# A chunked recurrence's 16x16 block inverses: from TensorE squarings to VectorE arithmetic through a DRAM scratch, with the grams of all head groups ahead

## The reference, cut to what matters

```python
def step(s, x):                       # s: one 64x64 state per head, 16 heads
    r, w, k, v, a, b = x              # one token
    sa = jnp.einsum("hij,hj->hi", s, a)
    s = s * w[:, None, :] + sa[..., None] * b[:, None, :] + v[..., None] * k[:, None, :]
    return s, jnp.einsum("hij,hj->hi", s, r)
```

## Time and profile before

| | |
|---|---|
| median of 3 runs | 1138.67 us |
| span of the profiled execution | 1140.1 us |
| TensorE busy | 1100.6 us, 97% |
| VectorE busy | 819.5 us, 72% |
| ScalarE busy | 574.0 us, 50% |
| recurrence, first half (groups 0 and 1) | 366.0 to 423.4 us |
| recurrence, second half (groups 2 and 3) | 423.4 to 476.4 us |

### The profile page before, as it was taken

One profiled execution on the slowest core, in us unless ns is written; L12 is line 12 of the kernel. 1 busy time (PEld: TensorE's weight loads), 2 busy tenths in 40 slices (PEclk: granted clock), 3 DMA queues, 4 the chain that ended last, 5 costly groups with the idle time before them and its releaser, 6 DMA issues.

```text
span 1140.1 us, 20465 instructions
## 1 busy us (share of the span) xinstructions
PE 1100.6 (97%) x8356; PEld 932.2 (82%) x8356; DVE 819.5 (72%) x1150; ACT 574.0 (50%) x736; POOL 42.0 (4%) x48
## 2 busy tenths in 40 slices
PE   9999999999999896899999999999999999999997
PEld 7888888889777586777888888798987788999996
DVE  4665554558398545878999997999999977555554
ACT  5645543355565443464433447456576656444443
POOL 0000000000001310100111100000000000000000
PEclk9999999999999989999999999999999999999999
DMA  9585555643243101287999964555440454555533
GB/s 330 192 264 185 176 178 198 215 161 122 94 132 125 48 21 42 85 274 253 356 344 350 354 226 140 165 179 185 149 160 14 155 182 143 185 193 175 204 128 112
DMA packets 129236, 204.89 MB, mean 180 GB/s; under 512 B 11192, under 2 KB 86733, under 8 KB 129166
## 3 DMA queue, kind: packets, MB, share of 16 engines
q1 hardware_dynamic: 121732, 176.58, 47.2%
q0 software_dynamic: 6560, 25.19, 6.4%
q10 hardware_dynamic: 874, 2.12, 0.5%
HBM read 201.78 MB, written 1.05 MB: 178 GB/s over the span
## 4 chain that ended last, share of the span: by engine, by line
PE 79%; DVE 13%; DMA 3%; ACT 3%; issue 2%; SPq 0%; ACTq 0%; DVEq 0%
PE ps L698 22%; PE ps L700 22%; PE ps L699 22%; PE ps L1144 3%; DVE wl L2532 2%; DVE wide L3219 2%; DMA raw<-in_ffn_w_up 2%; PE ps L924 1%; DMA raw<-in_ab_w_in 1%; PE ps L775 1%; PE ps L1057 1%; PE ps L1176 1%; PE ps L1449 1%; PE ps L1056 1%; PE ps L1081 1%
## 5 line engine op out<-in xcount | busy, mean ns | idle before, releaser
L2532 DVE TENSOR_TENSOR wl<-raw,wh 128x2048 fp32r<-128x2048 f32 (+2 forms) x154 | 345.3, 2247 | 97.5 <-ACT wh L1740 97.2
L698 PE MATMUL ps<-wh,xh 128*128 128x512 f32 (+3 forms) x856 | 335.7, 392 | 4.3 <-DVE wl L2532 2.3
L700 PE MATMUL ps<-wl,xh 128*128 128x512 f32 (+3 forms) x856 | 328.3, 384 | 0.0
L699 PE MATMUL ps<-wh,xl 128*128 128x512 f32 (+3 forms) x856 | 327.9, 383 | 0.0
L1740 ACT ACTIVATE wh<-raw 128x2048 fp32r<-128x2048 f32 (+2 forms) x154 | 287.0, 1878 | 52.6 <-PE ps L700 30.2
L698 PEld LDWEIGHTS ps<-wh,xh 128*128 128x128 f32 x856 | 160.9, 188 | 39.4 <-issue 3.4
L700 PEld LDWEIGHTS ps<-wl,xh 128*128 128x128 f32 x856 | 160.8, 188 | 31.8
L699 PEld LDWEIGHTS ps<-wh,xl 128*128 128x128 f32 x856 | 161.0, 188 | 30.2 <-issue 1.0
L698 PE MATMUL ps<-wh,gh 128*128 128x512 f32 x288 | 112.7, 391 | 0.8 <-DVE wl L2532 0.8
L699 PE MATMUL ps<-wh,gl 128*128 128x512 f32 x288 | 112.3, 390 | 0.0
L700 PE MATMUL ps<-wl,gh 128*128 128x512 f32 x288 | 112.1, 389 | 0.0
(11 more groups left out here) (423 smaller groups left out, 1367.7 us busy)
## 6 DMA issues: line engine op xcount, KB each, us to landing
wide<-in_w_ada POOLq DMA_DIRECT2D x24, 1024.0 KB, 10.1
raw<-in_ffn_w_gate SPq DMA_DIRECT2D x44, 512.0 KB, 4.3
raw<-in_ffn_w_up SPq DMA_DIRECT2D x44, 512.0 KB, 5.5
raw<-in_ffn_w_down SPq DMA_DIRECT2D x22, 1024.0 KB, 5.1
raw<-in_w_mlp_in SPq DMA_DIRECT2D x16, 1024.0 KB, 7.2
raw<-in_w_mlp_out SPq DMA_DIRECT2D x16, 1024.0 KB, 5.2
raw<-in_w_in SPq DMA_DIRECT2D x16, 512.0 KB, 4.9
raw<-in_w_in SPq DMA_DIRECT2D x8, 1024.0 KB, 5.1
```

What stands on the lines that cost most here:

```text
L698: pe.matmul(o, lh, rh, start=start, stop=False)
L699: pe.matmul(o, ll, rh, start=False, stop=False)
L700: return pe.matmul(o, lh, rl, start=False, stop=stop)
L2532: v.tensor_tensor(wl[:, s, 0:width], raw[:, s, 0:width], f32(wh[:, s, 0:width]), ALU.subtract).then_inc(lo_ready[s], 1)
```

## The change

- `power2` to `inverse` are gone on TensorE, and with them the copies of x2, x4, x8, t2, t4 and t8 on ScalarE and VectorE. Half of `gram_ts`'s second loop (16 matmuls a group) goes too.
- VectorE cuts the near blocks out of the gram (`near_blocks`: two masked products and a reduction). SyncE stores them to DRAM (`near_in`) and loads them back with one 16x16 block in each of 128 partitions, for two groups at once. VectorE inverts 128 blocks together (`near`: sizes 1, 2, 4, 8 in turn, 18 instructions). SyncE stores the result, loads it back by eight DMAs (`near_out`), and VectorE spreads it to `t8` (`inverse_out`).
- The flips, grams and masks of groups 2 and 3 come before the second part of groups 0 and 1. So groups 2 and 3 get buffers of their own (one in `xh`), ScalarE takes over their `bk_out`, and `near(1)` stands in VectorE's list after `y1_out(1)`.
- The gate products move behind the grams of all groups. The pieces of block 2 of `w_o` wait for other steps, and the last two of them are issued behind `near_out(1)`.

```diff
@@ SyncE @@
+                near_in(0)
                 a_columns((0, 1))
-                in_pieces(("o",) + O_ORDER[1], 0)
+                near_out(0)
+                near_in(1)
+                in_pieces(("o",) + O_ORDER[1], 0, (0, 1))
+                near_out(1)
+                in_pieces(("o",) + O_ORDER[1], 0, (2, 3))
                 a_columns((2, 3))
                 sp.wait_ge(S("gate_T"), B("gate_T") + 4)
                 in_pieces(("o",) + O_ORDER[2], 2)
-                for a, step in enumerate(("wkv.gkv", "wkv.x4", "wkv.t2", "wkv.t4")):
+                for a in pieces:
+                    step = ("wkv.gkv", "wkv.mt", "wkv.r1", "wkv.m2")[a]
+            def near_in(hh):
+                for g in (2 * hh, 2 * hh + 1):
+                    sp.wait_ge(S("wkv.nc"), B("wkv.nc") + g + 1)
+                    sp.dma_start(near_md[g].rearrange("u p c -> p u c"), WKV_TMP(W, raw, xh_plain)[g]["far"].rearrange("p (u c) -> p u c", u=8))\
+                      .then_inc(S("near_stored"), 16)
+                sp.wait_ge(S("near_stored"), B("near_stored") + 32 * (hh + 1))
+                if hh:
+                    sp.wait_ge(S("wkv.near"), B("wkv.near") + 1)
+                sp.dma_start(near_m[:, 0:256], near_md[2 * hh:2 * hh + 2].rearrange("g u (b s) c -> (g u b) (s c)", s=16)).then_inc(S("near_loaded"), 16)
+            def near_out(hh):
+                sp.wait_ge(S("wkv.near"), B("wkv.near") + hh + 1)
+                sp.dma_start(near_ud[2 * hh:2 * hh + 2].rearrange("g u (b s) c -> (g u b) (s c)", s=16), near_u[:, 0:256])\
+                  .then_inc(S("inverse_stored"), 16)
+                sp.wait_ge(S("inverse_stored"), B("inverse_stored") + 16 * (hh + 1))
+                for g in (2 * hh, 2 * hh + 1):
+                    if hh:
+                        sp.wait_ge(S("wkv.t8"), B("wkv.t8") + g - 1)
+                    for half in range(2):
+                        for y in range(2):
+                            a, b = 64 * half, 64 * (half ^ y)
+                            sp.dma_start(dst[a:a + 64, 4 * y:4 * y + 4, :], src[b:b + 64, 4 * y:4 * y + 4, :]).then_inc(S(f"inverse{g % 2}"), 16)
@@ TensorE @@
             for g in (0, 2):
-                for step in (flip, gram, gram_ts, power2, gram_v):
-                    step(g)
-                    step(g + 1)
-                power4(g)
...
-                for step in (fourth, inverse):
-                    step(g)
-                    step(g + 1)
+                flip(g)
+                flip(g + 1)
+                for x in range(2):
+                    gram(g, x)
+                    gram(g + 1, x)
+                gram_ts(g)
+                gram_ts(g + 1)
+                if g == 0:
+                    gram_v(0)
+                    gram_v(1)
+            gate_product(0, 0, 2)
+            gate_product(0, 1, 6)
+
+            for g in (0, 2):
+                if g == 2:
+                    gram_v(2)
+                    gram_v(3)
+                    pe.wait_ge(S("wkv.gkvc"), B("wkv.gkvc") + 3)
+                    next_state(0, 1)
                 off_block(g)
@@ ScalarE @@
+            ar_out(0)
+            ar_out(1)
+            gkv_out(0)
+            gkv_out(1)
+            for g in (2, 3):
+                ar_out(g)
+                bk_out(g)
+            gate_out(0, 0)
+            gate_out(0, 1)
...
                 r1_out(g + 1)
                 if g == 0:
+                    act.wait_ge(S("wkv.near"), B("wkv.near") + 2)
                     split_in_place(("o",) + O_ORDER[1])
@@ VectorE @@
+            def near_blocks(g):
+                v.wait_ge(S("wkv.gram_b"), B("wkv.gram_b") + g + 1)
...
+                for y in range(2):
...
+                    m = v.tensor_tensor(tmps[g]["xt"][:, 256 * y:256 * y + 256].rearrange("p (b q c) -> p b q c", b=2, q=2), x, diag, ALU.mult)
+                link(m)
+                v.tensor_reduce(tmps[g]["far"].rearrange("p (u c) -> p u c", u=8), tmps[g]["xt"].rearrange("p (u b c) -> p u c b", u=8, b=4),
+                                AX_X, ALU.add).then_inc(S("wkv.nc"), 1)
+            def near(hh):
+                v.wait_ge(S("near_loaded"), B("near_loaded") + 16 * (hh + 1))
...
+                for s in (4, 8):
+                    u11, u12, u22, m12 = corners(s)
...
+                    for a, b, o in ((m12, u22, part), (u11, part, u12)):
+                        for n in range(k):
+                            m = v.tensor_tensor(products[:, n], a[:, n].unsqueeze(2).to_broadcast([P, s, s, s]),
+                                                b[:, n].rearrange("p j c -> p c j").unsqueeze(1).to_broadcast([P, s, s, s]), ALU.mult)
+                        link(m)
+                        for n in range(k):
+                            m_ = v.tensor_reduce(o[:, n], products[:, n], AX_X, ALU.add)
...
+                m_.then_inc(S("wkv.near"), 1)
+            def inverse_out(g):
+                v.wait_ge(S(f"inverse{g % 2}"), B(f"inverse{g % 2}") + 64 * (g // 2 + 1))
...
+            bk_out(0)
+            bk_out(1)
             for g in (0, 2):
-                for step in (bk_out, mask_b, mask_x, mask_k, t1_out, y2_out):
+                for step in (near_blocks, mask_b, mask_k, mask_x):
                     step(g)
                     step(g + 1)
+                if g == 0:
+                    near(0)
+            inverse_out(0)
+            inverse_out(1)
...
                 y1_out(g + 1)
+                if g == 0:
+                    near(1)
```

More of the change, by code:

```diff
@@ L88, in constants @@
         "upto_st": j <= i,
+        "near": near,
         "incl_st": (r <= c) & same,
@@ L464, in sources @@
             return [(kblock(SRC[what], name[1] * 512, 512, name[2]), flat.rearrange("p (a n) -> p a n", a=4))]
+        near_md, near_ud = [nc.dram_tensor(n, (NG, 8, P, 16), F32).ap() for n in ("near_blocks", "near_inverses")]
         block = ctx.enter_context(nc.Block())
@@ L1163, in flip, with gram @@
                 m.then_inc(S("wkv.T"), 1)
-            def gram(g):
+            def gram(g, x):
                 pe.wait_ge(S("wkv.ar"), B("wkv.ar") + g + 1)
[L1168 to L1178, removed]
+                if g < 2:
+                    pe.wait_ge(S("wkv.bk"), B("wkv.bk") + g + 1)
+                else:
+                    pe.wait_ge(S("wkv.bka"), B("wkv.bka") + g - 1)
+                ar = tmps[g]["ar"].rearrange("p (q x c j) -> p q x c j", q=4, x=2, c=2)
+                for q in range(4):
+                    for c in range(2):
+                        for e in range(2):
+                            rows = slice(64 * e, 64 * e + 64)
+                            b0 = x * 512 + q * P + 64 * c
+                            m = pe.matmul(bank(g, 2 * x + e)[64 * c:64 * c + 64, q * P:(q + 1) * P],
+                                          tmps[g]["bk"][rows, b0:b0 + 64], ar[rows, q, :, c, :], start=True, stop=True)
+                m.then_inc(S(("wkv.gram_b", "wkv.gram_k")[x]), 1)
             def gram_ts(g):
@@ L1189, in gram_ts @@
                             o = 256 - 256 * e + q * CH
[L1190 to L1199, removed]
+                            m = pe.matmul(bank(g, e)[to:to + 64, o:o + CH], tmps[g]["ar"][rows, a0:a0 + 64],
+                                          tmps[g]["bk"][rows, b0:b0 + 64], start=True, stop=True)
                 m.then_inc(S("wkv.gram_ts"), 1)
[L1202 to L1206, removed]
             def gram_v(g):
                 pe.wait_ge(S("wkv.gk"), B("wkv.gk") + g + 1)
+                if g >= 2:
+                    pe.wait_ge(S("wkv.st"), B("wkv.st") + g - 1)
                 for p, e, q, half, to, j in units("gk"):
@@ L1386, in _ @@
                 else:
+                    pe.wait_ge(S("wkv.gkvc"), B("wkv.gkvc") + 4)
+                    next_state(0, 2)
                     from_states(0, 0)
@@ L2125, in step @@
                     act.wait_ge(S("wkv." + sem), B("wkv." + sem) + g + 1)
[L2126 removed]
+                    act.activation(tmps[g][dst][:, 0:n], bank(g, b)[:, 0:n], ACT.Copy).then_inc(S("wkv." + done), 1)
                 return step
@@ new lines, in inverse_out @@
+            def inverse_out(g):
+                v.wait_ge(S(f"inverse{g % 2}"), B(f"inverse{g % 2}") + 64 * (g // 2 + 1))
+                if g >= 2:
+                    v.wait_ge(S("wkv.r1"), B("wkv.r1") + g - 1)
+                shape = [P, 8, 4, 16]
+                v.tensor_tensor(tmps[g]["t8"].rearrange("p (u b c) -> p u b c", u=8, b=4),
+                                near_c[:, g % 2, :].rearrange("p (u c) -> p u c", u=8).unsqueeze(2).to_broadcast(shape),
+                                masks[:, MI["near"]:MI["near"] + CH].rearrange("p (b c) -> p b c", b=4).unsqueeze(1).to_broadcast(shape), ALU.mult)\
+                 .then_inc(S("wkv.t8"), 1)
@@ L2994, in step @@
                         v.wait_ge(S("wkv." + free), B("wkv." + free) + g + 1)
-                    v.tensor_tensor(eight(tmps[g % 2][dst]), eight(tmps[g % 2][src]), mask8("unit"), ALU.add).then_inc(S("wkv." + done), 1)
```

(4 more changed lines are left out.)

238 lines of the change are left out of this document (113 added, 125 removed), and 3 rows, old and new, of the table SHARED.

## The result

| | median us | lowest to highest | runs |
|---|---|---|---|
| before | 1139.14 | 1136.75 to 1143.59 | 4 |
| after | 1155.22 | 1151.84 to 1157.31 | 4 |

The ratio is 1.0135, with a 95% interval of 1.0109 to 1.0162: the change makes the kernel slower, by 15.2 us between the profiled spans and 16.1 us between the medians. The forecast was 1131 us, so it was wrong, and in its sign.

A forecast was written before the change was run, and what follows sets the result against it. TensorE, busy 97% of the span, was taken as the bound. The terms -24.8 + 9.5 + 4.7 + 3.0 make -7.6 us, so 1138.67 becomes 1131 us, range 1120 to 1139.

The forecast's parts named there:

- Nothing changes until group 0's b and k are copied: First half of the recurrence: timing stays as before until that copy ends at 369.8 us; no loss was priced.
- Everything behind the recurrence hangs on its end and moves with it: After the recurrence: later stages shift by the same amount and keep their distances; no term of its own.
- the prediction's own signs of being wrong: Pieces 3 and 4 landing before 412, a 64-byte-piece store over 5 us, or a later stage not moving with the recurrence's end.
- `near`, 5.6 us each: VectorE's block inversion: 18 instructions priced from profile rows at 5.6 us together, so near(0) ends at 385.4.
- `near(1)` from 401.5 to 407.1: First half: near(1) starts once the second gate product and y1_out(1) end, and takes 5.6 us.
- The wait that the change adds, 9.5 us: Before off_2(0): TensorE stands some 14.7 us for pieces queued behind near_out(1), a loss of 9.5 us.
- Second half, 24.8 us gained with 15.0 left: From the second half's start to off_2(2): 39.8 us shrinks to 15.0, including 1.8 us of issue gaps.
- The clock, 4.7 and 3.0 us: Half clock costs 4.7 us behind the stall (10 us long) and 3.0 us from a first fall under the gates.
- C: Rival, chance 0.15: four legs through DRAM each take 1 to 2 us more, giving 1135 to 1139 us.
- D: Rival, chance 0.09: slower, the same DRAM legs at the loaded queue's 5.9 us each, giving 1142 to 1145 us.
- B: Rival, chance 0.26: the clock falls less; 1128 us without the first fall, 1123 without any.
- E: Rival, chance 0.08: faster small loads and pieces, added wait's loss some 6 us instead of 9.5, giving 1118 to 1120 us.

The follow-up runs named there:

- e1: The changed kernel with its four new buffers allocated behind all others: 1144.76 us median, ratio 1.0047 to the kernel before.
- e2: The kernel before with one unused buffer of 3456 bytes per partition ahead of xh: 1152.39 us median, ratio 1.0111.
- e3: The changed kernel with new buffers allocated last, and pieces 3 and 4 of w_o block 2 issued ahead of near_out(1): 1135.03 us, ratio 0.9955.
- e4: The changed kernel with new buffers allocated last, and GpSimd's gated folds waiting for near(1): 1134.46 us, ratio 0.9944.
- e5_all_three: The changed kernel with buffers last, pieces 3 and 4 ahead of near_out(1), and gated folds behind near(1): 1127.03 us, ratio 0.9886.

## Why the prediction was wrong, step by step

- **"Nothing changes until group 0's b and k are copied" and "Everything behind the recurrence hangs on its end and moves with it".** This step failed, and it was in the text only as these sentences, with no term of its own. The four buffers ahead of xh put 3456 bytes in front of xh, xl, gh and gl, which then start 128 bytes past a multiple of 256. The traces show 4.8 us for it ahead of the recurrence and 7.1 behind, 11.9 us; e1 and e2 show 10 to 13 us by the medians and e1's span. It is the largest error, and no rival held it. One of the prediction's own signs of being wrong did: a later stage does not move with the recurrence's end.
- **`near`, 5.6 us each.** `near(0)` took 6.56 us: its products over 512 elements took 1.03 and 1.09 us, where I had used a pass over 512 at 0.7. `near_blocks` ahead of it took 1.72 us a group instead of 1.45, its reduction 1.02 instead of 0.68. `near(0)` ran from 379.4 to 386.0 us once the 4.8 us lost ahead are taken off; forecast were 379.8 to 385.4. `near(1)` took 13.5 us, because I priced VectorE alone and did not look at what GpSimd does at that time. Its folds stood in the trace of before in the same part of the program. The Trainium skill, "SBUF — State Buffer", section "Who interferes with whom", says that a VectorE instruction with two SBUF inputs contends with a GpSimd instruction that reads SBUF, and that the second to issue blocks until the first is done. The trace agrees: 0.17 us becomes 1.19 us beside operations of 1.27 us, and each ends just behind one of them. Two copies with a single SBUF input were slowed as well (1.01 and 1.21 us).
- **`near(1)` from 401.5 to 407.1.** It ran from 408.1 to 421.6, the 4.8 us taken off. 6.6 us late at its start. The gates and `off_block` ran at half clock from 397 us (0.51 there), which is some 3.8 us of it (see the clock, below). The folds are some 1.2: ScalarE's copy for the second y1 ended at 411.05, so with a y1 of 0.69 us behind it `near(1)` could have begun at 411.7 instead of 412.89. The gates began 0.8 us late, and some 0.8 us I did not locate.
- **The wait that the change adds, 9.5 us.** The mechanism was right. From the end of `near(1)` to `off_2(0)` I had 14.2 us (407.1 to 421.3); measured are 426.36 to 440.55, 14.2 us. That the two agree so well is in part luck: the store took 1.7 us where I had 2.3, the eight loads 5.3 instead of 5.8, the two pieces 4.7 instead of 3.6. `off_2(0)` came at 435.8 by the clock of before instead of 421.3, all of it inherited from the late end of `near(1)`. The loss was 24.0 us, where the terms for the wait and the first fall of the clock made 12.5, and e3 shows that the queue's order is worth about 10 of it.
- **Second half, 24.8 us gained with 15.0 left.** From `gram_v(2)` at 453.55 us to `off_2(2)` at 471.32 it took 17.8 us, so the gain was 22.0. Its issue gaps, 0.73, 1.33 and 0.80 us, make 2.9 us instead of the 1.8 I allowed; the other 1.7 us I did not locate. The term was mis-sized by 2.8 us.
- **The clock, 4.7 and 3.0 us.** Behind the stall the clock was low until about 445 us, some 4.3 us of work and not 10. From `off_2(0)` to the second half's start 13.0 us passed, against 11.7 in the kernel before, so it cost 1.3 us and not 4.7. The first fall came too, from about 397 to 407 us. From the first gate product to the product that the second y1 takes, 12.2 us passed (396.64 to 408.80), against 8.3 in e4 (392.15 to 400.49), where the clock was back at 394. That is 3.8 us, near the 3.0 forecast, and it is part of the late `near(1)`.
- **The sum.** Forecast -7.6; measured 4.8 ahead of the recurrence, 3.3 in it, 7.1 behind it, 15.2 together. Of the 22.8 us between the two, 11.9 are outside the recurrence. The 10.9 in it are 11.5 more before `off_2(0)`, 2.8 less gained in the second half, and 3.4 less lost behind the stall. With the buffers last, the queue mended and the folds moved, the change gives 13 to 14 us (e5_all_three: ratio 0.9886, and 1127.03 against 1141.16 us beside it).
- **The rivals.** C and D set their prices on the legs through DRAM. These were as estimated: stores 3.1 us, loads back 2.0 us, inverses 2.2 us in the median. D had the right sign, and the trace refutes its reason. The prediction's sentence on a doubled time for pieces under 512 B could not have applied as it stood: the row it starts from, of 256-byte pieces, is itself under 512 B. B is half true: the fall behind the stall cost 1.3 us, but the first fall came at full price. E is refuted by the eight loads, issued in 5.2 us, and by pieces that took longer than forecast.

## What to carry to other kernels

When a change adds a buffer, ask what lies behind it: keep operands that TensorE streams on multiples of 256 bytes (shown here for 128x512 products alone), or allocate the newcomer last. Price a VectorE step beside the GpSimd work of the same moment, not by its shortest row: many short linked operations suffer most, each waiting out a whole GpSimd one. When a result differs from a local forecast, take landmarks ahead of the change and behind it first; an offset that grows where nothing was changed is not the change's logic.

## What the runs showed that I had not expected

- A 128x512 product whose moving operand starts 64 or 128 bytes past a multiple of 256 bytes has a pitch of 232.5 to 233.3 ns instead of 227.5, some 2% of TensorE's time. Products of 256 columns with the shifted tensor as weight show no loss (281 ns against 283 in the mean).
- The same program part does not always bring the clock down: the kernel before had 0.50 at 399 to 402 us in its profile, and e2_before_padded, with the same instructions, held 1.00 from 380 to 450 us. Its profiled span is only 6.2 us above that of before, while the medians lie 13 us apart. The traces show where: e2 enters the recurrence 4.8 us late and leaves it 1.3 us early (477.01 us against 478.32, at the same product in both). Its four runs point at the clock too: 1148.46, 1150.41, 1154.37 and 1156.49 us at mean granted clocks of 0.998, 0.996, 0.993 and 0.990; at 0.998 the kernel before took 1136.44 to 1138.75.
- After a wait of 23.9 us the clock was back at 1.00 some 4.3 us into the work; in the kernel before the low stretch under the gates lasted about 10 us.
